# A product over the whole array added to every tile of the second gated-linear-attention loop

## What is computed

```python
def gla_scan(q, k, v, log_a, s0):
    ...
    def step(state, inp):
        qi, ki, vi, gi = inp
        b = jnp.cumsum(gi, axis=2)
        b_end = b[:, :, -1:, :]
        q_dec = qi * jnp.exp(b)
        k_dec = ki * jnp.exp(-b)
        a = jnp.where(tri, jnp.einsum('bhtk,bhsk->bhts', q_dec, k_dec), 0.0)
        o = jnp.einsum('bhts,bhsv->bhtv', a, vi) + jnp.einsum('bhtk,bhkv->bhtv', q_dec, state)
        k_to_end = ki * jnp.exp(b_end - b)
        state = jnp.exp(b_end[:, :, 0, :])[..., None] * state + jnp.einsum('bhsk,bhsv->bhkv', k_to_end, vi)
        return state, o
```

## Time and profile before

| what | value |
|---|---|
| median of 3 runs (lowest, highest) | 5070.39 us (5068.37, 5077.62) |
| the profiled execution: its own time | 5066.31 us |
| its span, first to last instruction | 5064.5 us |
| TensorE busy, share of the span | 4320.9 us, 85% |
| VectorE, ScalarE busy | 42%, 26% |
| mean granted clock of TensorE over the span | 0.898 |
| second loop, first layer (18 tiles) | 59.32 us from its first product to the meeting of the engines |
| second loop, second layer (16 tiles) | 53.60 us |

### The profile page before, as it was taken

One profiled execution on the slowest core, in us unless ns is written; L12 is line 12 of the kernel. 1 busy time (PEld: TensorE's weight loads), 2 busy tenths in 40 slices (PEclk: granted clock), 3 DMA queues, 4 the chain that ended last, 5 costly groups with the idle time before them and its releaser, 6 DMA issues. The chain is left out here.

```text
span 5064.5 us, 65113 instructions
## 1 busy us (share of the span) xinstructions
PE 4320.9 (85%) x25386; PEld 3416.4 (67%) x25386; DVE 2136.3 (42%) x4404; ACT 1301.0 (26%) x3065; POOL 428.5 (8%) x399
## 2 busy tenths in 40 slices
PE   5898998699578859989969957793999998988899
PEld 2787897476357727878956735582777776767677
DVE  3211010365756541111016666575372045657554
ACT  3100111265411030001115633113111146661211
POOL 1100000200001020000010000103241000100100
PEclk7899999899659979999989976796999999999999
DMA  4112114402115431211171020432112114236411
GB/s 175 49 69 89 61 59 131 168 14 83 37 44 194 156 145 59 79 75 72 47 228 51 14 100 19 174 137 113 66 61 79 63 46 130 94 119 244 160 66 64
DMA packets 199825, 485.41 MB, mean 96 GB/s; under 512 B 41560, under 2 KB 92504, under 8 KB 186780
## 3 DMA queue, kind: packets, MB, share of 16 engines
q1 hardware_dynamic: 186080, 433.79, 24.3%
q0 software_dynamic: 13440, 47.46, 2.5%
HBM read 312.61 MB, written 168.57 MB: 95 GB/s over the span
## 5 line engine op out<-in xcount | busy, mean ns | idle before, releaser
L72 PE MATMUL tm_tacc<-tm_tw_hi,hT_hi 128*128 128x384 f32 (+1 forms) x1120 | 409.8, 366 | 40.4 <-DVE tm_tw_lo L410 30.2
L73 PE MATMUL tm_tacc<-tm_tw_lo,hT_hi 128*128 128x384 f32 (+1 forms) x1120 | 405.9, 362 | 0.0
L74 PE MATMUL tm_tacc<-tm_tw_hi,hT_lo 128*128 128x384 f32 (+1 forms) x1120 | 405.9, 362 | 0.0
L72 PE MATMUL tz_tacc<-tz_tw_hi,hT_hi 128*128 128x512 f32 x896 | 360.5, 402 | 37.2 <-DVE tz_tw_lo L410 27.2
L72 PE MATMUL cm_acc<-hT_hi,cm_wb_hi 128*128 128x512 f32 (+1 forms) x912 | 341.9, 375 | 20.2 <-DVE cm_wb_lo L317 20.2
L74 PE MATMUL tz_tacc<-tz_tw_hi,hT_lo 128*128 128x512 f32 x896 | 356.7, 398 | 0.0
L73 PE MATMUL tz_tacc<-tz_tw_lo,hT_hi 128*128 128x512 f32 x896 | 356.7, 398 | 0.0
L73 PE MATMUL cm_acc<-hT_lo,cm_wb_hi 128*128 128x512 f32 (+1 forms) x912 | 341.4, 374 | 0.0
L74 PE MATMUL cm_acc<-hT_hi,cm_wb_lo 128*128 128x512 f32 (+1 forms) x912 | 341.0, 374 | 0.0
L407 DVE CAST tm_tw_hi<-tm_traw 128x512 fp32r<-128x512 f32 (+1 forms) x64 | 48.8, 762 | 512.1 <-PE tm_tacc L74 477.5
L72 PEld LDWEIGHTS tm_tacc<-tm_tw_hi,hT_hi 128*128 128x128 f32 x1120 | 211.0, 188 | 75.0 <-DVE tm_tw_lo L410 35.1
(11 more groups left out here) (324 smaller groups left out, 8603.8 us busy)
## 6 DMA issues: line engine op xcount, KB each, us to landing
scr_z<-tz_tz SPq DMA_DIRECT2D x112, 256.0 KB, 2.0
ada_w<-in_w_ada SPq DMA_DIRECT2D x16, 1536.0 KB, 17.7
scr_zcm<-cm_zo SPq DMA_DIRECT2D x18, 1152.0 KB, 5.1
scr_ztm<-tm_tz SPq DMA_DIRECT2D x68, 256.0 KB, 2.0
out_mx<-scr_mix SPq DMA_DIRECT2D x34, 512.0 KB, 4.4
out_gt<-scr_ztm SPq DMA_DIRECT2D x34, 512.0 KB, 5.7
scr_xres<-out_x POOLq DMA_DIRECT2D x34, 512.0 KB, 2.9
nt_xb<-scr_xres SPq DMA_DIRECT2D x8, 2048.0 KB, 10.4
```

Of the source, the lines that this page charges most:

```text
L72: nc.tensor.matmul(out, ah, bh, start=start, stop=False)
L73: nc.tensor.matmul(out, ah, bl, start=False, stop=False)
L74: return nc.tensor.matmul(out, al, bh, start=False, stop=stop)
```

## The change

Behind each tile's `outputs` in the second loop TensorE gets one more matmul: `perm` (128 x 128) as the stationary operand, the first 256 columns of `q`, 128 rows, as the moving one, into the first 256 columns of bank 6 or 7 in turn. It is f32 like its neighbours, waits for no semaphore and raises none, and nothing reads the result. It runs 18 times in the first layer and 16 times in the second.

```diff
@@ -1075,6 +1075,7 @@
                     if n + 1 < NO:
                         products(NO + n + 1)
                     outputs(NO + n)
+                    nc.tensor.matmul(bank[6 + n % 2][:, 0:256], perm[:, :], q[:, 0:256], start=True, stop=True)
 
             @block.vector
             def _(dve):
```

## The result

The changed kernel took 5100.78 us (median of 4 runs, 5096.45 to 5105.28), the kernel before 5070.31 beside it: a ratio of 1.0058, with an interval of 1.0040 to 1.0075. It became slower by 30 us, where 19 us less was forecast. It is the first rival: in the profiled execution (5100.19 us) the clock did not rise in either loop before its last product.

What follows compares the result with a forecast made beforehand. TensorE at half clock was taken to bound the second loop. Three tiles per layer at +0.89 us, the other intervals at -0.88 and -1.9 at each loop's end summed to -19.6 us: 5051 us, range 5040 to 5066.

Steps and rivals of the forecast that it cites:

- the first rival: Second loop: the clock never rises and every product is paid in full, +27 us, 5098 us; chance 0.10.
- the loop is bound by TensorE at half clock: Second loop: TensorE busy 55.69 of 59.32 us at clock 0.50, a tile every 3.10 us, 1.76 at full clock.
- The price of the product: Added matmul in each second-loop tile: 0.89 us at half clock, 0.46 us at full clock.
- L974's 9 units: Products of 16 rows at half clock: 10 halves, 9 units of 512 columns, in 8.04 us, giving 0.89 us a unit.
- the clock would rise: Second loop: a full-array product per tile lifts the clock from 0.50 to 1.00 after three half-clock tiles per layer.
- The row that I held nearest: At 3096.46 one such tile at half clock, then 128 x 128 transposes from 3099.56; clock 1.00 from 3100.30.
- the clock holds once up: Second loop: a raised clock stays, as it did from 3103.70 to 3111.00 with TensorE busy 6.16 of 7.30 us.
- the other engines keep up: Second loop at 2.22 us a tile: VectorE's turn of 1.3 us and ScalarE's 0.60 us are covered by TensorE's work.
- the last interval: End of the second loop: 2.62 us shrinks to 1.68 at full clock, 0.94 less.
- The number of tiles at half clock: Second loop: three tiles per layer before the clock rises, 1 to 5 likeliest, giving 5058 to 5044 us; chance 0.65.

Runs made afterwards that it cites:

- e2: The change with its added product at 512 columns but only 16 rows, against the kernel before: 5125.77 us, ratio 1.0116.
- e12: As e5, plus a tiny product of 64 rows and 8 columns between the added product and L1030: 5104.27 us, ratio 1.0078 against the kernel before.
- e3: The kernel before plus three full-array products of 512 columns per layer in the wait ahead of the second loop, none in it: 5028.35 us, ratio 0.9924.
- e1: The change with its added product at 512 columns instead of 256, against the kernel before: 5060.33 us, ratio 0.9982.
- e4: The change with its added product at 384 columns instead of 256, against the kernel before: 5056.07 us, ratio 0.9978.
- e5: The change's 256-column product moved one line earlier, between products and outputs, ahead of L1030: 5037.46 us, ratio 0.9933 against the kernel before.
- e7: The change with a 512-column product behind outputs in every second tile only, against the kernel before: 5050.02 us, ratio 0.9957.
- e6: The burst of e3 ahead of the second loop plus the change's 256-column product in each tile: 5043.97 us, ratio 0.9942 against the kernel before.
- e10: As e5, ahead of L1030, with 128 columns instead of 256: 5050.41 us, ratio 0.9960 against the kernel before.
- e9: The change's 256-column product moved inside outputs, behind L1030 and ahead of L1038: 5049.26 us, ratio 0.9957 against the kernel before.

## Why the prediction was wrong

*That the loop is bound by TensorE at half clock*: right. The added time lengthened the tiles in full, in e2 and e12 too, and at full clock a bare tile takes 1.75 us (forecast 1.76, e3).

*The price of the product*: too small. Forecast 0.89 at half clock and 0.46 at full clock, measured 1.15 and 0.63. Both rows that I took the earlier trace rows are of long runs of one kind, which spread the fixed part over many products; the added one stands alone between 64-row work. The row had it: L974's 9 units took 8.04 us, and at the 0.855 a unit that e1 and e4 give they are 7.7 us of columns. I divided the rest by nine instead of charging it once for each tile. With 1.15 the first rival comes to 30 x 1.15 + 0.7 = 35 us, which is what the loops show (35.0).

*That the clock would rise*: wrong, and this is the step that turned the sign. I forecast 0.50 for three tiles and then 1.00; it was 0.50 over 75.93 us, up to the loop's last product. The row that I held nearest, a tile at half clock and then transposes, differs from the change in a way that the experiments show to matter: its transposes followed each other from 3099.56 to 3103.01 with no product of another footprint between them, where the change has one piece of 1.15 us between 64-row work in each tile. (The rise itself came 0.7 us into them, right behind a tile of 64-row work, so the row doesn't say how much of them it took.) I argued with amounts (0.7 us of transposes there, 0.89 here in each tile) and took the amount as sufficient. The experiments show that with the amount unchanged, its place decides: behind `outputs` never before the loop's last product (change), ahead of L1030 after 8.7 us (e5), and mostly not with an 8-column product between (e12); and that more columns (e1, e4) or denser pieces (e7) also suffice. The two errors may be one: the 0.30 us that I left out of the price is time that its columns don't account for, and it recurs in each tile. That is argued and not shown; e12 speaks against its simplest form (below).

*That the clock holds once up, and that the other engines keep up*: right. It held to the end of the loops in e3, e5 and e6, and in e5 and e6 TensorE waited for no engine after the loop's first tile; at e3's 1.75 us it waited in one tile of each layer, and in the last one. At full clock the last interval was 1.68 us in e5, as forecast. Where I wrote that TensorE needs 2.2 us a tile at full clock, it is 2.38 (e6).

*The number of tiles at half clock*, k = 3: in the kernels whose clock rose it was 1 to 8 (both in e10), 2 to 5 in most. The two layers of one execution differ too. The gain that I had summed for the change (19 us) was reached by products in other places: 35 (e5, 25 of it in the profiled loops), 22 (e9), 21 (e10, half of the columns).

*Rival 1* had the mechanism and the right side. I gave it 0.10. What should have raised that: the loop's 64-row work fills the queue and never lifts the clock in 57 us, so the added product alone had to carry the rise, with no row of a piece so short and so often interrupted that did it.

What stays open is what the clock answers to in this mix. e5 and the change have the same products and differ in the changeovers and in the length of the tile (3.95 and 4.25 us); e12 and e5 differ in both as well. A plain count of full-array work per time doesn't order the runs: e12 spreads it over 4.56 us a tile, more than the change's 4.25, and yet rose in one layer. Whether the length of an undisturbed piece of such work decides, or the moment at which the loop begins has a part in it, no run separates.

## What to carry to other kernels

A loop of products on parts of the array can keep TensorE fully busy at half clock; look for a busy share near 1 beside a granted clock of 0.50. If its own work holds a clock that is up, as here, don't pay in the loop: put a dense burst over the whole array into a wait just ahead of it, and make it long enough that it does so in every execution (with three products the gain was 41 us and four executions lay within 7 us; with two it was left to chance). If a product must go into the loop, put it beside one with the same footprint: in e5's place the change's product gained 35 us instead of losing 30.

## What the runs showed of the hardware

- A product over the whole array that stands alone between 64-row products pays a fixed part beside its columns: 0.30 us at half clock, 0.20 at full clock, for 256, 384 and 512 columns alike. Ahead of a product with the same 128 x 128 footprint it pays nothing of the 0.30 (e5: 3.95 - 3.10 = 0.85, the bare columns), behind one 0.06 (e9). A product of 8 columns with 64 rows takes 0.31 itself, and 0.61 with what the two of the same footprint that it separates pay again (e12).
- The weights of a product with the same footprint were loaded 0.36 us ahead of it, during the product before; those of a product with another footprint only from its own start (the change, L1030 and L1019).
- TensorE's occupation doesn't tell its clock: 91.64 us busy of 92.20 at 0.50 with 16-row products (e2), 43.20 of 43.20 at 1.00 with products of the same length over 128 rows (e1).
- The same tile work ran at 0.50 for whole loops and at 1.00 for whole loops, with the clock at which it began (before, and e3).
